# Differential attention: scores in two banks in place of four, half turns, and two banks for the values' result

## The reference

```
def one_block(args):                      # one block of 128 queries, all heads
    qblk, i = args
    qpos = i * Q_BLOCK + jnp.arange(Q_BLOCK)
    s = jnp.einsum('bqhcd,bkhcd->bhcqk', qblk, kf) * scale      # c: the two sub-heads
    dist = qpos[:, None] - kpos[None, :]
    bias = -slopes[:, None, None] * dist.astype(jnp.float32)
    s = s + bias[None, :, None]
    s = jnp.where((dist >= 0)[None, None, None], s, jnp.finfo(jnp.float32).min)
    p = jax.nn.softmax(s, axis=-1)
    a = p[:, :, 0] - lam * p[:, :, 1]
    return jnp.einsum('bhqk,bkhe->bqhe', a, vf)                 # then rms_norm over e
```

## Time and profile before

| | us |
|---|---|
| median of the runs | 1733.21 |
| the profiled execution | 1736.92 |
| its span in the trace | 1735.6 |
| PE busy | 1674.9 (97%) |
| DVE busy | 967.1 (56%) |
| ACT busy | 740.7 (43%) |
| GpSimd busy | 672.9 (39%) |
| stage of the change | 199 to 372 |

### The profile page before, as it was taken

How to read it: one execution, slowest core, us unless ns; L and a number is a source line. 1 busy time by engine, 2 the same in 40 slices (tenths; PEclk the granted TensorE clock), 3 DMA queues, 4 the chain that set the end, 5 groups by cost and what they waited for, 6 DMA issues and landing times.

```text
span 1735.6 us, 25677 instructions
## 1 busy us (share of the span) xinstructions
PE 1674.9 (97%) x9958; PEld 1377.3 (79%) x9958; DVE 967.1 (56%) x1976; ACT 740.7 (43%) x1474; POOL 672.9 (39%) x291
## 2 busy tenths in 40 slices
PE   8999999899999999999999999999999999999987
PEld 6789777688888888888878888867777888896766
DVE  4797545453223165555497133565666667975463
ACT  5222355553323454444323443265666335225552
POOL 3787322243334455444476511211113323522331
PEclk9999999999999999999999989999999999999999
DMA  8565312132224313333465412100000533221121
GB/s 244 147 193 166 96 49 65 45 110 85 62 85 145 110 49 109 98 97 98 119 206 149 124 31 66 49 26 26 14 26 2 157 101 91 85 62 44 50 67 49
DMA packets 255160, 156.08 MB, mean 90 GB/s; under 512 B 6018, under 2 KB 251071, under 8 KB 255039
## 3 DMA queue, kind: packets, MB, share of 16 engines
q1 hardware_dynamic: 252238, 147.78, 29.1%
q10 hardware_dynamic: 2800, 6.65, 1.2%
HBM read 152.32 MB, written 2.10 MB: 89 GB/s over the span
## 4 chain that ended last, share of the span: by engine, by line
PE 87%; DVE 5%; ACT 2%; issue 2%; POOL 1%; SPq 1%; DMA 1%; ACTq 0%; DVEq 0%
PE ps L807 69%; PE ps L2466 3%; PE ps L2497 3%; PE ps L2480 2%; POOL w_lo L777 1%; PE ps L1581 1%; PE ps L1597 1%; PE ps L1543 1%; DVE mod_sums_odd L1528 1%; DVE probsT L2577 1%; SPq L1189 1%; PE ps L1589 1%; ACT w_hi L718 1%; PE ps L2251 1%; PE ps L2201 0%
## 5 line engine op out<-in xcount | busy, mean ns | idle before, releaser
L777 POOL TENSOR_TENSOR w_lo<-w_raw,w_hi 128x1024 fp32r<-128x1024 f32 (+1 forms) x220 | 589.9, 2686 | 849.6 <-ACT w_hi L718 849.3
L807 PE MATMUL ps<-h_hi,w_lo 128*128 128x512 f32 x1088 | 438.8, 403 | 8.9 <-DVE h_lo L1126 2.9
L807 PE MATMUL ps<-h_hi,w_hi 128*128 128x512 f32 x1088 | 425.8, 391 | 0.0
L807 PE MATMUL ps<-h_lo,w_hi 128*128 128x512 f32 x1088 | 425.2, 391 | 0.0
L807 PEld LDWEIGHTS ps<-h_hi,w_lo 128*128 128x128 f32 x1088 | 205.4, 189 | 57.8 <-issue 4.9
L718 ACT ACTIVATE w_hi<-w_raw 128x1024 fp32r<-128x1024 f32 (+1 forms) x220 | 228.8, 1045 | 38.2 <-PE ps L807 20.9
L807 PEld LDWEIGHTS ps<-h_hi,w_hi 128*128 128x128 f32 x1088 | 205.0, 188 | 44.3
L807 PEld LDWEIGHTS ps<-h_lo,w_hi 128*128 128x128 f32 x1088 | 205.7, 189 | 42.4 <-issue 2.4
L2550 ACT ACTIVATE probs<-probs,small 128x512 f32<-128x512 f32 (+3 forms) x128 | 93.7, 732 | 29.6 <-DVE small L2566 29.0
L1528 DVE SCALAR_TENSOR_TENSOR mod_sums_odd<-mod_raw,small,mod_sums_odd 128x256 f32<-128x256 f32 x154 | 96.9, 695 | 0.5
L2577 DVE COPY probsT<-ps 128x256 f32<-128x256 f32 (+3 forms) x128 | 55.1, 430 | 66.8 <-PE ps L2480 65.9
(11 more groups left out here) (426 smaller groups left out, 3281.5 us busy)
## 6 DMA issues: line engine op xcount, KB each, us to landing
w_raw<-in_w_in SPq DMA_DIRECT2D x56, 512.0 KB, 5.1
mod_raw<-in_mod_w SPq DMA_DIRECT2D x24, 1024.0 KB, 6.5
w_raw<-in_w_up SPq DMA_DIRECT2D x44, 512.0 KB, 3.8
w_raw<-in_od_w_in SPq DMA_DIRECT2D x28, 512.0 KB, 3.7
w_raw<-in_ev_w_in SPq DMA_DIRECT2D x20, 512.0 KB, 3.8
w_raw<-in_w_down SPq DMA_DIRECT2D x16, 512.0 KB, 4.0
w_raw<-in_w_mem_kv SPq DMA_DIRECT2D x8, 512.0 KB, 4.0
w_raw<-in_w_attn_branch SPq DMA_DIRECT2D x8, 512.0 KB, 3.9
```

What stands on the lines that cost most here:

```text
L777: POOL.tensor_tensor(wlo[:, p, 0:n], raw[:, p, 0:n], f(whi[:, p, 0:n]), ALU.subtract).then_inc(*chunk_lo.by(c))
L807: ins = PE.matmul(out, l, r, start=first and n == 0, stop=last and n == 2)
```

## The change

The scores of every unit go to banks 2 and 3, in place of 2 and 3 for even and 4 and 5 for odd units, and the scores of unit s wait for `d_maxed(s - 1)`. The turn becomes two transposes of 64 rows for each 128 keys, the upper half of the queries into bank 4 and the lower into bank 5; ACT's copy reads both banks in one instruction and puts the halves side by side in `aT`. The values' result alternates between banks 6 and 7, and its matmuls wait for `d_out(u - 2)`.

```diff
     def d_bank(u, c):
-        return 2 + 2 * (u % 2) + c
-
-    d_out_bank = bank(7, P)
+        return 2 + c
+
+    def d_out_bank(u):
+        return bank(6 + u % 2, P)
...
-                if s >= 2:
-                    PE.wait_ge(*d_maxed(s - 2))
+                if s >= 1:
+                    PE.wait_ge(*d_maxed(s - 1))
...
                 for k in range(i + 1):
-                    ins = PE.transpose(bank(6, P, k * P), sc2[u % 3][:, 0, k * P:(k + 1) * P], ident[:])
+                    for half in range(2):
+                        rows_, own = halves_turned(half)
+                        ins = PE.transpose(bank(4 + half, HEAD, k * HEAD), sc2[u % 3][rows_, 0, k * P:(k + 1) * P], own)
...
                 PE.wait_ge(*d_copied(u))
-                if u >= 1:
-                    PE.wait_ge(*d_out(u - 1))
+                if u >= 2:
+                    PE.wait_ge(*d_out(u - 2))
                 for k in range(i + 1):
-                    ins = PE.matmul(d_out_bank, aT[u % 2][:, k * P:(k + 1) * P], vt[:, k, e * P:(e + 1) * P],
+                    ins = PE.matmul(d_out_bank(u), aT[u % 2][:, k * P:(k + 1) * P], vt[:, k, e * P:(e + 1) * P],
...
-                ACTE.activation(aT[u % 2][:, 0:n], bank(6, n), ACT.Copy).then_inc(*d_copied.by(u))
+                both = ps[:, 4 * 512:6 * 512].rearrange("p (h e) -> p h e", h=2)[:, :, 0:n // 2]
+                ACTE.activation(aT[u % 2][:, 0:n].rearrange("p (k h q) -> p h k q", h=2, q=HEAD),
+                                both.rearrange("p h (k q) -> p h k q", q=HEAD), ACT.Copy).then_inc(*d_copied.by(u))
...
-                DVE.tensor_scalar(qT[:, e, i * P:(i + 1) * P], d_out_bank, d_stats(u)[:, 4:5], None,
+                DVE.tensor_scalar(qT[:, e, i * P:(i + 1) * P], d_out_bank(u), d_stats(u)[:, 4:5], None,
```

## The result

The changed kernel takes 1758.18 us (median of 4 runs, 1753.17 to 1761.06) beside 1732.76 (1732.25 to 1733.23) for the kernel before: a ratio of 1.0149, 95% interval 1.0135 to 1.0162, so 25.4 us slower. The forecast was 1758 us, slower.

What follows compares the result with a forecast made beforehand. PE, busy 97% of the span, was taken to bound the kernel. Terms 20.2 + 1.4 - 1.9 - 5.2 = +14.5 us, +24.5 with the clock, on 1733.2 gave 1758 us, range 1744 to 1769.

Steps and rivals of the forecast that it cites:

- The wait of the scores: Scores wait for the previous unit's maximum, behind DVE's eviction, at ten steps outside "mem": +20.2 us, bounds 18.8 to 23.
- The "mem" pieces: Stretch at 326 to 344 us where ACT and DVE set the pace; scores now wait too: +1.4 us, bounds 0 and 3.
- The clock: Five to six long PE waits followed by half clock, +9 us, and +1 in "mem": +10, bounds 0 and +19.
- Others set the pace: In "mem", PE's waits before scores grow towards 3 us, but other engines set the pace, so clock costs only +1.
- The half turns: Shorter turns save 2.5 us, less change of array form 3.2, less 0.5 in "mem": -5.2, bounds 0 and -6.
- The second bank: Second bank for the values' result removes some of 5.8 us of PE waits: -1.9 us, bounds 0 and -5.8.
- clock holds: Rival: the new waits come but PE's clock stays at 1.00 throughout the stage: 1748 us (1744 to 1752), chance 0.27.
- The other side: Rival: the maximum is done before PE reaches the scores in every step, saving 7.1 us: 1726 us, chance 0.04.

Runs made afterwards that it cites:

- filled kernel: Changed kernel with 4 to 6 matmuls of unread results put ahead of each of the 13 waits for the maximum: 1748.3 us, ratio 1.0086.
- early kernel: Changed kernel with DVE taking the maximum of unit s at the end of its step s: 1722.8 us (0.9944), again 1727.1 us (0.9968).
- early_full: Changed kernel with maxima at the end of DVE's step s and half turns undone (full 128x128 turns into bank 4): 1724.8 us, ratio 0.9955.

## Why the prediction was right

*The wait of the scores* was priced at 20.2 us, from DVE's starts. Its ten places outside "mem" idle for 19.4 us in the changed kernel (17.7 for the nine, 1.73 for step 31), which with the 0.07 by which idle time reads shorter is 20.1. Places and sizes were right, since DVE's order did not change and its chain could be read off the old trace as it would be; only who waits for it was new. The steps without an eviction had no wait, as read at step 16.

*The "mem" pieces* were given +1.4. At full clock, in the filled kernel, they take 19.1 us from the last "qm" piece (340.59) to the first "km" matmul (359.68), in place of 17.8 (326.42 to 344.18): +1.3. PE's idle time before the scores there, 7.6 us in the changed kernel, would have misled: ACT and DVE set the pace, and PE stood idle there before the change too.

*The clock* was given +10: 9 for five to six waits and 1 in "mem". The filled kernel makes it 10.9. In "mem", where 1 was given, it is 3.1: the same stretch takes 22.2 us in the changed kernel (348.62 to 370.78) and 19.1 in the filled one. The 7.8 left for five stretches are 1.6 each, the size read at 881 us. "Others set the pace" was too good for "mem": once scores stand behind the maximum, scores, turn, values and m_diag matmuls lie on the chain one after the other. The chain shows it at steps 29 and 30, in the changed kernel (first fence) and in the filled one (second):

```profile
359.58 1.23 PE ps L1582 x4
...
363.06 0.57 ACT m_hi L1746
...
365.60 1.11 PE ps L1582 x4
...
370.09 0.69 issue
```
```profile
351.44 0.70 PE ps L1588 x4
...
353.45 0.57 ACT m_hi L1752
...
355.98 0.92 PE ps L1588 x4
...
358.90 0.78 issue
```

From the scores to the end of PE's part it takes 3.48 and 4.49 us in place of 2.01 and 2.92, which is 3.0 of the 3.1.

*The half turns* were sized at 5.2 and measured 1.7 to 2.6; this is the term that was off most. The first part of it (2.5 for the shorter turns) about holds. The second, 3.2 for a change of form saved between scores and turn, does not. The timeline of the changed kernel at full clock:

```profile
254.62 0.92 PE L1582 MATMUL ps<-k_T,q_T 64*128 64x384 f32 x4
255.37 0.41 PE L1592 MATMUL ps<-ident,diff_s 64*128 64x64 f32 x8
255.71 0.94 PE L1600 MATMUL ps<-v_tok,diff_aT 128*128 128x128 f32 x6
256.40 0.48 PE L807 MATMUL ps<-h_hi,w_lo 128*128 128x512 f32 x1
```

Against the earlier trace rows the scores do take 0.75 us to the turn in place of 0.85, and the turn 0.34 in place of 0.49. But the values take 0.69 to the next matmul, and took 0.59 before (283.41 to 284.00): the change from 64-row to 128-row form is still paid, now behind the turn. Of 0.25 saved, 0.15 is left. Read in the same way in the early kernel and in early_full, whole steps take 0.78 in place of 0.84, 1.28 in place of 1.39, 1.78 in place of 1.93 and 2.03 in place of 2.04: 0.33 for a head, 2.6 for eight. The stages at equal half clock give 1.7. The Trainium skill (page "TensorE: Matmul & The Clock Gate", section "LDWEIGHTS (loading the stationary operand)") says that a load of fewer rows takes as long as a full one, and for the single load the trace agrees: 138 ns with 64 rows in the filled kernel, 141 with 128 before, where the page's formula gives 107. The estimate made from it, that 160 loads would add 8.6 us, is not borne out: eight half turns, loads included, take 0.34 us to the next start, four full ones 0.49, so the loads overlap.

*The second bank* (-1.9) agrees with what is left, but was not measured by itself beside the new waits: at full clock 20.1 + 1.3 - 1.9 and the half turns at 2.6 make 16.9, at 1.7 they make 17.8, and the filled kernel's stage is 16.9 longer. Where the scores no longer wait it is worth 4.2.

So the sum hit in part by luck. For the stage it gave +24.5 us, and the stage grew by 27.9: by the steps the half turns saved 2.6 us less than counted, and the clock cost 0.9 more. The median grew by 25.4 only. In the profiled pair the rest of the kernel, which was to stay unchanged, was 3.8 us shorter, and nothing in the forecast stood for that. With the half turns at their measured size the forecast would have been 1760 to 1761.

The rival "clock holds" gave 1748, and the filled kernel, in which it does hold, takes 1748.3, with the same error in the half turns. The other side's mechanism (the maximum done before PE arrives) became true in the early kernel, at 1722.8 and 1727.1 on two chips, where 1726 was given.

## What to carry to other kernels

A buffer is free when its reader is done, and the reader's place in its own engine's order decides when: before giving away a second buffer, read in the old trace when the last read of it ends against when the writer comes back, at each kind of step, not on average. Where the new wait is behind another engine's eviction, moving that engine's read ahead of it can cost nothing and make the change pay: the same banks added 25 us in one order and, with the other, the kernel is 5 to 10 us faster than before. Look then at what the moved work delays; here it was `m_diag`. And price a PE wait of some 2 us with the clock behind it, here 1.6 us more for about half of them.

## What was not expected of the hardware

Waits of the same length were not alike. In the changed kernel 1.73 us (ended 211.22) and 1.99 (301.15) were followed by half clock, 1.73 (274.03) and 1.98 (250.41, 339.54) not. The wait of 1.83 us for `h_lo` in the earlier trace rows, followed by half clock before, stands in the changed kernel at 1452.22 with the same length, and no half clock behind it; in the second profiled execution of the changed kernel it has the same length and half clock behind it (from 1451.5). The pattern within the stage repeated to 0.1 us in two executions of the same kernel, though. What decides it stays open. With matmuls in about half of each of the 13 waits the clock was 1.00 behind all of them.
